# The last recurrent block takes the order of the others, and the splits for the output product move between exponentials and roots

## What is computed

```python
def rglru_block(xn, h0, conv_buf, w_in, conv_w, conv_b, gr_w, gr_b, gi_w, gi_b, lam, w_out):
    u = xn @ w_in
    gate, xb = u[..., :D_RNN], u[..., D_RNN:]
    xc, new_buf = causal_dwconv(xb, conv_buf, conv_w, conv_b)
    xblk = xc.reshape(B, T, N_LRU_BLOCKS, LRU_BW)
    r = sigmoid(einsum('btnc,ncd->btnd', xblk, gr_w) + gr_b)
    i = sigmoid(einsum('btnc,ncd->btnd', xblk, gi_w) + gi_b)
    log_a = -C_GATE * r * softplus(-lam)
    a = exp(log_a)
    b = sqrt(-expm1(2.0 * log_a)) * (i * xc)
    hs, h_last = lru_scan(a, b, h0)          # h_t = a_t * h_{t-1} + b_t
    y = (gelu(gate) * hs) @ w_out
```

## Time and profile before

| | us |
|---|---|
| time, median of 3 runs | 2496.83 |
| the 3 runs | 2494.64, 2496.83, 2498.89 |
| profiled execution, its own time | 2496.31 |
| span of the profiled execution | 2494.5 |
| PE busy | 2463.8 |
| block 3's gelu tile 0 starts on PE | 230.08 |
| second unit pair of the output product starts on PE | 299.03 |

### The profile page before, as it was taken

The page is one execution under the profiler, slowest core; times in us unless marked ns, Lnnn a source line. Parts: engine busy times, 40 slices in busy tenths (PEclk is TensorE's granted clock), DMA queues, the critical chain, the costliest instruction groups (busy, mean ns, idle before and its releaser), DMA issues.

```text
span 2494.5 us, 39868 instructions
## 1 busy us (share of the span) xinstructions
PE 2463.8 (99%) x15287; PEld 2410.2 (97%) x15287; DVE 1231.6 (49%) x1999; ACT 773.8 (31%) x1266; POOL 271.1 (11%) x388
## 2 busy tenths in 40 slices
PE   8999999999999999999999999999999999999999
PEld 8999899999999999999999867999999999999999
DVE  6666545533542553444566575355335424434542
ACT  6554533212311321112344675333112212211221
POOL 3212520000000000001220253200000000000000
PEclk9999999999999999999999999999999999999999
DMA  4111111111111111111382202111111111111112
GB/s 126 43 50 44 43 43 48 41 38 51 44 38 53 42 44 40 51 42 38 119 136 47 70 1 98 51 43 40 42 53 42 39 49 46 38 46 49 44 36 91
DMA packets 227189, 130.95 MB, mean 52 GB/s; under 512 B 24789, under 2 KB 224669, under 8 KB 226876
## 3 DMA queue, kind: packets, MB, share of 16 engines
q1 hardware_dynamic: 224948, 126.47, 17.3%
q10 hardware_dynamic: 2100, 3.37, 1.1%
q0 software_dynamic: 64, 0.05, 0.0%
HBM read 116.76 MB, written 15.01 MB: 53 GB/s over the span
## 4 chain that ended last, share of the span: by engine, by line
PE 95%; DVE 2%; ACT 1%; issue 1%; POOL 0%; DMA 0%; DVEq 0%; POOLq 0%; ACTq 0%
PE ps L874 30%; PE ps L876 30%; PE ps L875 30%; PE ps L1230 1%; PE ps L1282 1%; PE ps L1147 0%; PE ps L1330 0%; PE ps L861 0%; PE ps L1140 0%; PE ps L1331 0%; PE ps L1332 0%; PE ps L1060 0%; PE ps L1115 0%; DVE pt L2398 0%; DVE y L2380 0%
## 5 line engine op out<-in xcount | busy, mean ns | idle before, releaser
L874 PE MATMUL ps<-sa,whi 128*128 128x384 f32 (+1 forms) x1836 | 600.6, 327 | 1.2 <-DVE wlo L1909 1.2
L876 PE MATMUL ps<-sa,wlo 128*128 128x384 f32 (+1 forms) x1836 | 599.3, 326 | 0.0
L875 PE MATMUL ps<-sa,whi 128*128 128x384 f32 (+1 forms) x1836 | 598.9, 326 | 0.0
L874 PE MATMUL ps<-sb,whi 128*128 128x384 f32 (+1 forms) x1764 | 581.8, 330 | 0.0
L876 PE MATMUL ps<-sb,wlo 128*128 128x384 f32 (+1 forms) x1764 | 576.4, 327 | 0.0
L875 PE MATMUL ps<-sb,whi 128*128 128x384 f32 (+1 forms) x1764 | 575.8, 326 | 0.0
L1391 ACT ACTIVATE whi<-raw 128x1024 fp32r<-128x1024 f32 (+1 forms) x204 | 201.4, 988 | 874.3 <-PE ps L876 855.5
L874 PEld LDWEIGHTS ps<-sa,whi 128*128 128x128 f32 x1836 | 344.9, 188 | 2.4 <-issue 1.7
L875 PEld LDWEIGHTS ps<-sa,whi 128*128 128x128 f32 x1836 | 344.9, 188 | 0.3
L876 PEld LDWEIGHTS ps<-sa,wlo 128*128 128x128 f32 x1836 | 344.8, 188 | 0.0
L874 PEld LDWEIGHTS ps<-sb,whi 128*128 128x128 f32 x1764 | 331.8, 188 | 2.7 <-issue 1.2
(11 more groups left out here) (352 smaller groups left out, 2557.1 us busy)
## 6 DMA issues: line engine op xcount, KB each, us to landing
raw<-in_f_w_up SPq DMA_DIRECT2D x96, 512.0 KB, 3.8
raw<-in_f_w_down SPq DMA_DIRECT2D x64, 384.0 KB, 3.4
raw<-in_a_w_in SPq DMA_DIRECT2D x16, 512.0 KB, 3.9
x_spill<-x SPq DMA_DIRECT2D x1, 4352.0 KB, 15.0
x<-x_spill SPq DMA_DIRECT2D x8, 544.0 KB, 5.5
xrows<-in_x_prompt SPq DMA_DIRECT2D x8, 512.0 KB, 6.6
raw<-in_a_w_out SPq DMA_DIRECT2D x8, 512.0 KB, 3.9
raw<-in_w_q SPq DMA_DIRECT2D x16, 256.0 KB, 3.7
```

The costliest lines, as they stand in the source:

```text
L874: pe.matmul(out, whi[s][:, w], mhi[k][:, chunk(c)], start=(k == 0), stop=False)
L875: pe.matmul(out, whi[s][:, w], mlo[k][:, chunk(c)], start=False, stop=False)
L876: last = pe.matmul(out, wlo[s][:, w], mhi[k][:, chunk(c)], start=False, stop=(k == nk - 1))
```

## The change

Block 3 becomes a third turn of the loop's order for PE and SP. Its second gelu unit goes behind the gates, as `unit(4 * c + 3, 1, KD, split_a)`. On ACT the block is still written out, since more is in it: the casts of row tiles 0 to 5 move from between the gelus and gates to three other places: chunk 0 behind the exponentials, chunk 1 behind the first root, chunk 2 behind the second gelu tile. Each waits until PE has finished that chunk of the second gelu unit, since this unit still reads split_a. The six first pieces of the output product are done in another order. Scratch tiles move (sc4f to xcf).

```diff
-            def lru_block(c, first=False, both=False):
+            def lru_block(c, first=False):
                 ...
                 unit(4 * c + 1, 0, KD, split_a)
-                if both:
-                    unit(4 * c + 1, 1, KD, split_a)
                 pe.wait_ge(xc_lo, 2 * c + 2)
                 for m in range(2):
-                    for s, n in ((0, 4 * c + 2), (1, 4 * c + 2)) if both else ((1, 4 * c + 1), (0, 4 * c + 2)):
+                    for s, n in ((1, 4 * c + 1), (0, 4 * c + 2)):
                 ...
-                if not both:
-                    unit(4 * c + 3, 1, KD, split_a)
+                unit(4 * c + 3, 1, KD, split_a)
-            with pe.Fori(1, LRU_BLOCKS - 1) as c:
+            with pe.Fori(1, LRU_BLOCKS) as c:
                 lru_block(c)
-            lru_block(LRU_BLOCKS - 1, both=True)
...
-            for c in range(3):
-                for s in range(2):
-                    out_part(s, c, range(KD - 2))
+            for s, c in ((0, 0), (0, 1), (1, 0), (1, 1), (0, 2), (1, 2)):
+                out_part(s, c, range(KD - 2))
...
                 def highs(ch):
+                    act.wait_ge(bank_ready[3 + ch], 4 * c + 4)
                     for k in range(KD - 2):
...
                 for m in range(2):
+                    if last:
+                        highs(m)
+                        if m == 1:
+                            prep(4 * c + 4, 1, KD * P)
                     act.wait_ge(one_a2, 2 * c + m + 1)
                     act.activation(block_input(m), block_input(m), ACT.Sqrt).then_inc(root_ready, 1)
-                if not both:
-                    branch(1, 4 * c + 3, lambda: prep(4 * c + 4, 1, KD * P))
+                branch(1, 4 * c + 3, None if last else lambda: prep(4 * c + 4, 1, KD * P))
+                if last:
+                    highs(2)
...
             for k in range(KD - 2, KD):
                 act.wait_ge(z_ready, k + 1)
-                act.wait_ge(hlast_done, k + 1)
                 act.activation(split_a[0][k], z[:, k, :], ACT.Copy).then_inc(z_hi, 1)
```

More of the change, by code:

```diff
@@ L169, in build @@
         xcf = at("xcf", [P, 4, T], F32, reg_b + KD * T * 4)
-        sc4f = at("sc4f", [P, 4, T], F32, reg_c)
         xrows = at("xrows", [P, 9, D], F32, reg_b)
@@ L338, in gate_tiles @@
             if isinstance(c, int) and c == LRU_BLOCKS - 1:
-                return convin[:, 8:8 + T], sc4f[:, 1, :]
+                return convin[:, 8:8 + T], xcf[:, 0, :]
             return tuple(z[:, ds(2 * c + 2 + i, 1), :].rearrange("p o t -> p (o t)") for i in range(2))
@@ L346, in block_input, with root_scratch @@
             return (rstd, y)[m][:, :]
-        def root_scratch(m, last=False):
-            return sc4f[:, 3 - m, :] if last else xcf[:, 2 + m, :]
+        def root_scratch(m):
+            return xcf[:, 2 + m, :]
         def blocks(ap):
@@ L636, in conv_loads, with lru_loads @@
                     load(4 * c, s, w_cols(w_in, D + c * 256 + s * P), KD * P)
-            def lru_loads(c, both=False):
+            def lru_loads(c):
                 if not isinstance(c, int) or c > 0:
@@ L683, in _ @@
                            .then_inc(sink_in, 16)
-            with eng.Fori(1, LRU_BLOCKS - 1) as c:
+            with eng.Fori(1, LRU_BLOCKS) as c:
                 lru_loads(c)
-            lru_loads(LRU_BLOCKS - 1, both=True)
             with eng.Fori(0, KD // 2) as i:
@@ L1483, in lru_block @@
             def lru_block(c, first=False, last=False):
-                both = last
                 for s in range(2):
                     n, kt = 4 * c, 2 * c + s
-                    if s == 0 or both:
+                    if s == 0:
                         prep(n + 1, s, KD * P)
@@ L1517, in branch @@
                                        ACT.Gelu_apprx_tanh).then_inc(bank_free[b], 1)
-                        if ch == 1:
+                        if ch == 1 and prepare:
                             prepare()
-                        if last and s == 1:
-                            highs(ch)
                 def tanh(m):
                     kt = 2 * c + m
-                    act.activation(root_scratch(m, last), gate_tiles(c, m)[0], ACT.Tanh, scale=sp[:, 0, ds(kt, 1)])\
+                    act.activation(root_scratch(m), gate_tiles(c, m)[0], ACT.Tanh, scale=sp[:, 0, ds(kt, 1)])\
                        .then_inc(tanh_done, 1)
@@ L1530, in lru_block @@
                 branch(0, 4 * c + 1, lambda: prep_gates(4 * c + 2, 0))
-                if both:
-                    branch(1, 4 * c + 1, lambda: prep_gates(4 * c + 2, 1))
                 act.wait_ge(stash_done, 2 * c + 2)
@@ L1537, in gate_places @@
                 def gate_places(m):
-                    if both:
-                        return ((0, 4 * c + 2 + m, C_RB), (1, 4 * c + 2 + m, C_IB))
                     return ((1, 4 * c + 1 + m, C_RB), (0, 4 * c + 2 + m, C_IB))
@@ L1544, in lru_block @@
                     kt = 2 * c + m
-                    for i, (t, (s, n, col)) in enumerate(zip(gate_tiles(c, m), gate_places(m))):
+                    for t, (s, n, col) in zip(gate_tiles(c, m), gate_places(m)):
                         for ch in range(3):
@@ L1553, in lru_block @@
                                 prep(n + 1, s, KD * P)
[L1554 to L1557, removed]
+                act.wait_ge(bank_free[5], 4 * c + 3)
                 act.wait_ge(bank_free[2], 4 * c + 4)
-                if not both:
-                    apart()
-                    tanh(0)
-                    tanh(1)
+                apart()
+                tanh(0)
+                tanh(1)
                 for m in range(2):
@@ L2034, in lru_block @@
                          (3 * s, 3 * s + 1, 3 * s + 2), n,
-                         lambda: prep(n + 1, s, KD * P) if s == 0 or both else prep_gates(n + 1, 1),
+                         lambda: prep(n + 1, s, KD * P) if s == 0 else prep_gates(n + 1, 1),
                          CONV_IN[s], block_input(s))
@@ L2046, in lru_block @@
                 prep_gates(4 * c + 2, 0)
[L2047 to L2050, removed]
+                prep(4 * c + 3, 1, KD * P)
                 def gated(m):
-                    dve.wait_ge(bank_free[5 if both else 2], 4 * c + 3 + m)
+                    dve.wait_ge(bank_free[2], 4 * c + 3 + m)
                     tb = gate_tiles(c, m)[1]
@@ L2062, in decay @@
                     seq.settle()
-                    dve.scalar_tensor_tensor(yb, yb, 1.0, root_scratch(m, last), ALU.add, ALU.mult).then_inc(one_a2, 1)
+                    dve.scalar_tensor_tensor(yb, yb, 1.0, root_scratch(m), ALU.add, ALU.mult).then_inc(one_a2, 1)
                     first1 = requests(ta[:, SEQ:T])[:, :, 0]
@@ L2081, in lru_block @@
                 gated(0)
[L2082 to L2086, removed]
+                prep(4 * c + 4, 0, KD * P)
                 gated(1)
@@ L2093, in lru_block @@
                     scan(1)
-                    if not both:
-                        prep(4 * c + 4, 1, KD * P)
+                    prep(4 * c + 4, 1, KD * P)
                     return
@@ L2102, in mixed @@
                     for b in range(3):
-                        dve.wait_ge(bank_free[3 * m + b], 4 * c + 2)
+                        dve.wait_ge(bank_free[3 * m + b], 4 * c + 2 + 2 * m)
                     dve.tensor_tensor(z[:, kt, :], z[:, kt, :], gate_tiles(c, m)[1], ALU.mult).then_inc(z_ready, 1)
```

## The result

The changed kernel takes 2502.01 us (median of 20 runs), the one before 2495.22 (20 runs). The ratio is 1.0024, 95% interval 1.0018 to 1.003: slower by 4.5 to 7.5 us. The forecast was 5.2 us slower. The profiled execution took 2503.62 us, span 2501.8.

What follows compares the result with a forecast made beforehand. PE, busy 99%, bounds the kernel; DVE and POOL alternating put the last low part at 294.0, plus 10.2 us on PE gives 304.2 against 299.03, +5.2. From 2496.31 that gives 2501.5, stated as 2502.0 us, range 2493 to 2506.5.

Steps and rivals of the forecast that it cites:

- PE's order: Block 3 on PE: gates start at 241.94, second gelu unit ends at 265.66, the 1.8 us sigmoid wait goes.
- ACT: ACT in block 3: second exponential ends at 261.70, casts ready by about 276, added table load hidden.
- The port: SBUF port shared by DVE and POOL in block 3: they alternate, so shared work lasts the sum; last low part at 294.0.
- The sum of 30.7 us: Work from 263.3 to 294.0: DVE's 17.0 us plus 18 POOL subtractions at 0.76, 13.7 us.
- Behind it: PE after the last low part: last step 0.44, piece (1, 2) 2.64, 36 products 5.93, weights wait 1.16; 10.2 us.
- second chain: PE's own chain behind chunk 1's last low part at 283.1: arrives at 293.3, 0.7 us ahead of chunk 2's last low part.
- a times a: DVE's product reading one tile twice also excludes POOL by the skill's rule: 1.28 us; otherwise 2500.7 instead of 2502.0.
- the marker: First plain unit of the output product on PE: forecast at 304.2 against 299.03 before, +5.2 us.
- side by side: Rival: POOL and DVE run together, subtractions at 0.98 us; PE ends at 293.2, 5.8 us faster, 2491.0 us; chance 0.18.
- Partial exclusion: Rival: some DVE instructions, a*a or scans, let POOL through; +4 to -1 us, about 2499; chance 0.17.
- slower still: Rival: POOL at 0.98 us or PE at 1.2 GHz in the last 36 products; +1.7 to +4, about 2505; chance 0.13.
- the 5.0 us bound: Smallest difference from no change that a measurement can tell, about 0.2%; the forecast 5.2 us lay right on it.

Runs made afterwards that it cites:

- e1: Changed kernel with each of POOL's 18 subtractions replaced by two memsets that only write, low parts zero; 2489.5 us against 2496.37 before the change.
- e3: Changed kernel with 6 extra unread PE products ahead of each low-part wait in pieces (0, 0) and (0, 1); single run 2501.48 us.
- e4: Changed kernel with the output product's first six pieces in the old order; single run 2504.85 us.
- e2: Changed kernel with the 18 subtractions on DVE instead of POOL, chunks 0 and 1 ahead of the first scan; 2492.23 us against 2496.37 before the change.
- e6: Changed kernel, DVE doing the second weight early, then waiting for POOL's chunks 0 and 1 before the first scan; 2498.27 us against 2496.47 before the change.
- e5: Kernel before the change with its 18 subtractions on DVE instead of POOL, in the same place; 2496.37 us against 2496.47.

## Why the prediction was right

- *PE's order.* Gates from 241.94, the second gelu unit to 265.66, no wait for a sigmoid: as forecast. The waits of 1.8 and 2.8 us went.
- *ACT.* Second exponential out at 261.60 (forecast 261.70), last cast at 275.60 (276).
- *The port.* DVE's second product of `decay` ended at 263.22 (263.3), chunk 1's last low part at 283.17 (283.1), the last of all at 293.43 (294.0). The sum of 30.7 us measures 30.2. e1 shows that the cause is reading side by side: beside writes of nearly the same busy time on POOL (0.84 us for each, 0.98 before) the DVE products keep their 1.28 us and PE waits for no low part.
- *Behind it, and here the path was another.* The forecast had PE waiting for chunk 2's last low part, with its own chain 0.7 us ahead. PE did not wait: it came 0.47 us late. The second chain's sum was short by one step: five steps of piece (0, 2) stand ahead of the last, not four, which makes it 293.7 and not 293.3. It came at 293.90, and the low part, with 293.43, was 0.6 early. From there 10.4 us follow and not 10.2: the 36 products take 6.16 us for 5.93 (e3 and e4 have 6.14).
- *Luck.* The low part 0.6 us early and 0.7 us more behind it (10.87 for 10.2) cancel at the marker. That 2502.0 met the median of 2502.01 is luck too: it started from a median of 2496.83 over three runs, which is 2495.22 over 20, and left out the 2 us behind the marker.
- *a times a.* The one point that only the rule of the Trainium skill covered ("SBUF — State Buffer", Who interferes with whom): DVE's product at 265.02, which reads one tile twice, made POOL's subtraction of 265.04 take 2.13 us. It counts. So its 1.28 us belonged in the sum. The time alone could not tell 2502.0 from 2500.7.
- *Missed within the sum.* The two one-input scalings of 8 columns (TENSOR_SCALAR) were not in it; 0.17 us each alone (e2), 0.35 together. Yet the sum came out 0.5 short of the forecast: with DVE's 17.0 and these 0.35 taken from the measured 30.2, the 18 subtractions took 12.9 us, 0.71 each and not 0.76. The six of 320 columns are shorter (0.87 for 1.00 alone), which is part of it.
- *The size.* 5.3 us at the marker. The timed difference, 6.8 us between the medians, 4.5 to 7.5 by the interval, holds it. Two other sets of runs of the kernel before have medians 1.2 us above the one used here, so a part of the 6.8 is spread between sets.

The rivals: side by side is what e1 shows (291.90 at the marker, for the rival's 293.2), but only with POOL's reads taken away. Partial exclusion is ruled out, as each kind of instruction took its turn, scans and a*a too. Of *slower still* a small part came: the lower clock brought PE 0.47 us late to the last low part, worth 0.3 us against e3, but the last 36 products ran at full clock and the turns were no slower. For the forecast's chances: the result lay beyond the 5.0 us bound, on the side that had 0.44.

What stays open: why the 36 products of tiles 6 and 7 take 6.14 us at full clock and not the 5.93 of half a unit, and how the 2192.9 to 2200.4 us behind the marker come about.

## What to carry to other kernels

Ask of every piece of work that is moved what else reads at that time, not only whether its own engine is free: here a slot on POOL was free only while DVE had next to nothing to do, or while POOL only wrote. Where they must overlap, try the work on the engine that does a piece in less time (e2), and let the side go first that has more work waiting behind it (e6). A wait on an engine that is not the bound can bring the end forward. And when two chains come close in a forecast, count the steps of both: here the chain that was put 0.7 us ahead of the other came 0.5 us behind it and set the end.

## What the runs showed of the hardware

- DVE and POOL took turns in the changed kernel, one instruction each, however short, while both had work and POOL read: a product of 8 columns that takes 0.16 us alone took 0.85 to 0.98 beside POOL's subtractions. Four such products and two scalings stood in this chain.
- DVE's TENSOR_SCALAR on 8 columns, with one input, was held up as well: 0.94 and 0.95 us beside POOL's subtractions, and 0.49 and 0.22 beside POOL's memsets in e1 (0.17 alone, as in e2). Two-input products beside memsets were not held up.
- PE's waits of 1.0, 0.7 and 0.4 us in e2 left the mean clock at 1.00 over the stretch from 264.31 to 292.38. One wait of 2.83 us in e5 was followed by 10.18 us to the marker, one of 2.80 before by 8.80, at mean clocks of 0.70 and 0.82.
